# Gate and up products of a gated layer as seven half-size products for eight, in a two-block transformer kernel

## What is computed

```python
def swiglu_ffn(h, w1, w3, w2):
    return (jax.nn.silu(h @ w1) * (h @ w3)) @ w2

    # D_MODEL = 1024, SEQ = 512, D_FF_2 = 2816, two layers
    h = h + swiglu_ffn(rmsnorm(h, norm_ffn_g[layer]), ffn_w1[layer], ffn_w3[layer], ffn_w2[layer])
```

## Time and profile before

| | |
|---|---|
| median of 3 runs | 1737.45 us (1736.9 to 1738.46) |
| span of the profiled execution | 1736.2 us |
| PE busy | 1723.5 us, 99% of the span |
| DVE busy | 817.1 us, 47% |
| ACT busy | 688.5 us, 40% |
| POOL busy | 740.6 us, 43% |
| first gated layer, its stretch on the chain | 359.04 us |
| second gated layer, the same | 342.74 us |

### The profile page before, as it was taken

The page is one execution under the profiler, slowest core; times in us unless marked ns, Lnnn a source line. Parts: engine busy times, 40 slices in busy tenths (PEclk is TensorE's granted clock), DMA queues, the critical chain, the costliest instruction groups (busy, mean ns, idle before and its releaser), DMA issues.

```text
span 1736.2 us, 23746 instructions
## 1 busy us (share of the span) xinstructions
PE 1723.5 (99%) x8050; PEld 1418.5 (82%) x8050; DVE 817.1 (47%) x1457; ACT 688.5 (40%) x1041; POOL 740.6 (43%) x329
## 2 busy tenths in 40 slices
PE   9999999999999999999999999999999999999998
PEld 7877778888888788888888888888888888888887
DVE  5655565333333678532332335566665523323425
ACT  5566553222222434632322224565655432322324
POOL 3232325444446297444354353442424353443441
PEclk9999999999999999999999999999999999999999
DMA  7442223322222133233233233231212332332231
GB/s 199 113 102 79 73 65 117 98 97 97 97 97 97 61 116 107 84 101 97 85 109 97 85 109 97 74 97 48 87 58 74 97 110 85 98 107 85 97 96 49
DMA packets 153686, 162.25 MB, mean 93 GB/s; under 512 B 10628, under 2 KB 114680, under 8 KB 153632
## 3 DMA queue, kind: packets, MB, share of 16 engines
q1 hardware_dynamic: 149167, 158.66, 29.7%
q10 hardware_dynamic: 4464, 2.89, 0.5%
HBM read 157.84 MB, written 3.67 MB: 93 GB/s over the span
## 4 chain that ended last, share of the span: by engine, by line
PE 95%; DVE 2%; ACT 1%; issue 0%; DMA 0%; SPq 0%; DVEq 0%; ACTq 0%
PE ps L1295 83%; PE ps L1316 2%; PE ps L1751 1%; PE ps L1643 1%; PE ps L1324 1%; PE ps L1514 1%; PE ps L1533 1%; DVE ps L2279 1%; PE ps L1426 0%; PE ps L1420 0%; PE ps L1784 0%; PE ps L1497 0%; PE ps L1430 0%; PE ps L1742 0%; PE ps L1498 0%
## 5 line engine op out<-in xcount | busy, mean ns | idle before, releaser
L640 POOL TENSOR_TENSOR wlo<-raw,whi 128x1024 fp32r<-128x1024 f32 x228 | 550.2, 2425 | 765.9 <-ACT whi L730 750.9
L1295 PE MATMUL ps<-h_hi,wlo 128*128 128x512 f32 x1376 | 546.1, 397 | 0.8 <-DVE gv L2045 0.3
L1295 PE MATMUL ps<-h_hi,whi 128*128 128x512 f32 x1376 | 536.6, 390 | 0.0
L1295 PE MATMUL ps<-h_lo,whi 128*128 128x512 f32 x1376 | 536.2, 390 | 0.0
L730 ACT ACTIVATE whi<-raw 128x1024 fp32r<-128x1024 f32 x282 | 292.7, 1055 | 503.7 <-PE ps L1295 495.1
L1295 PE MATMUL ps<-m_hi,wlo 128*128 128x512 f32 x800 | 314.5, 393 | 0.0
L1295 PE MATMUL ps<-m_hi,whi 128*128 128x512 f32 x800 | 311.5, 389 | 0.0
L1295 PE MATMUL ps<-m_lo,whi 128*128 128x512 f32 x800 | 311.4, 389 | 0.0
L1295 PEld LDWEIGHTS ps<-h_hi,whi 128*128 128x128 f32 x1376 | 258.3, 188 | 55.1
L1295 PEld LDWEIGHTS ps<-h_hi,wlo 128*128 128x128 f32 x1376 | 258.5, 188 | 54.2 <-issue 1.6
L1295 PEld LDWEIGHTS ps<-h_lo,whi 128*128 128x128 f32 x1376 | 258.6, 188 | 51.1 <-issue 0.5
(11 more groups left out here) (311 smaller groups left out, 1621.1 us busy)
## 6 DMA issues: line engine op xcount, KB each, us to landing
raw<-in_ffn_w SPq DMA_DIRECT2D x264, 256.0 KB, 2.8
raw<-in_w_ff SPq DMA_DIRECT2D x128, 256.0 KB, 2.8
raw<-in_hg_w_in SPq DMA_DIRECT2D x64, 256.0 KB, 3.1
raw<-in_w_in SPq DMA_DIRECT2D x40, 256.0 KB, 5.2
raw<-in_cp_w_in SPq DMA_DIRECT2D x24, 256.0 KB, 2.9
raw<-in_w_out SPq DMA_DIRECT2D x16, 256.0 KB, 2.9
raw<-in_cp_w_out SPq DMA_DIRECT2D x16, 256.0 KB, 2.9
raw<-in_hg_w_out SPq DMA_DIRECT2D x16, 256.0 KB, 2.9
```

The source lines that it names most:

```text
L640: pool.tensor_tensor(wlo[:, u % RING, :, :], raw[:, u % RING, :, :], whi[:, u % RING, :, :].bitcast(F32), ALU.subtract).then_inc(unit_lo, 1)
L1295: mm = pe.matmul(ps[:, b, :], wt[:, s, a, m * P:(m + 1) * P], xt[:, kts[a], :], start=starts and a == 0 and i == 0, stop=last)
```

## The change

The first two groups stay as they were. From the third on, gate and up of each group are a block each (18 blocks per layer). A block multiplies a 1024 x 256 weight matrix with 1024 x 512 tokens. Both are cut in half both ways, and with Strassen's algorithm (Winograd's form) seven half-size products give what eight gave. Each product has a contraction of 4 tiles, 128 features and 256 tokens: 12 matmuls of 128 x 256, 84 for a block where 48 of 128 x 512 stood.

- Tokens: normalised once, ahead of the first drain (`normed_tokens`), and three or four differences and sums of halves made, split into `t_hi`, `t_lo` and into parts of `m_hi`, `m_lo`, `h_hi`, `h_lo` (the old contents are done with by then).
- Weights: DVE makes four sums for each block (`weight_sum`) and now the seven low parts (`low`, 128 x 512 each). ACT makes the seven high parts. POOL makes only the low parts of the down weights (`down_low`). High and low parts stand in 12 slots of 128 x 512.
- Sums of the products: banks 0 to 3 take one product each in turn; ACT copies the first (`y1`), DVE adds the others from PSUM into `u2`, `u3`, `u4`, `gate` and `ghid` in pieces of 128 x 256. The fifth product is accumulated in PSUM onto the first.
- Down: two groups' down products are summed in PSUM (`down_pair`), so that `xT` is added to once for two groups; the group left over goes alone at the end.
- The norm's matmuls move ahead, to the middle of the second unit of the first group, and ACT's work for the norm ahead of its unit copies.

```diff
+FORMS = 7
+TAGS = ("y1", "u2", "u3", "p5", "c11", "c12", "c21")
+SUM_OF = {1: 2, 2: 3, 3: 1, 5: 4}
+HALF = SEQ // 2
+SLOTS = 12
+BLOCKS = 2 * (GLU_GROUPS - 2)
+PAIRS_IN_LOOP = 3
+LATER_UNITS = 8 + 2 * BLOCKS + 4 * (PAIRS_IN_LOOP + 1)
+N_LOOP, N_TURN = 2 * FORMS + 1, 4 * FORMS + 8
...
+def block_banks(j):
+    at = [(b - j) % 4 for b in (0, 1, 2, 3, 0, 1, 2)]
+    return [((tag, j), b) for tag, b in zip(TAGS, at)]
...
+                def down_low(n0, d0, i=None):
+                    for d in range(8):
+                        n = n0 + d
+                        s = form_slot(layer, n)
+                        u = first + (10 if n0 < N_LOOP else 22) + d // 2
+                        pool.wait_ge(form_hi, at(i, N_TURN, SLOTS_USED * layer + n + 1))
+                        pool.tensor_tensor(lo_slot(s), raw[:, u % RING, d % 2, :], hi_slot(s).bitcast(F32), ALU.subtract)\
+                            .then_inc(down_lo, 1)
...
+                def slot_free(n, i):
+                    if n < 4:
+                        act.wait_ge(tokens_lo, FORMS * layer + 4)
+                    elif n < SLOTS:
+                        act.wait_ge(unit_begun, first + 6 + (n - 4) // 2)
+                    else:
+                        act.wait_ge(form_used, at(i, N_TURN, (SLOTS_USED - 1) * layer + n - SLOTS + 1))
...
@@ -1682,25 +2052,78 @@
...
+                def products(j, slots_before, i=None):
+                    for f in range(FORMS):
+                        s = form_slot(layer, block_slot(j) + f)
+                        b = part_bank(layer, j, TAGS[f])
+                        x_hi, x_lo = rounded_tokens(f)
+                        pe.wait_ge(form_lo, at(i, 4 * FORMS, FORMS * (BLOCKS * layer + j) + f + 1))
+                        if j == 0:
+                            pe.wait_ge(tokens_lo, FORMS * layer + f + 1)
+                        pe.wait_ge(drained[b], part_nth(layer, j, i, TAGS[f]) - 1)
+                        for k in range(4):
+                            for p, (wt, xt) in enumerate(((lo_slot(s), x_hi), (hi_slot(s), x_lo), (hi_slot(s), x_hi))):
+                                begins, ends = k == 0 and p == 0, k == 3 and p == 2
+                                mm = pe.matmul(ps[:, b, 0:HALF], wt[:, k * P:(k + 1) * P], xt[:, k, :],
+                                               start=begins and TAGS[f] != "c11",
+                                               stop=ends, skip_group_check=TAGS[f] == "c11")
+                                if begins and f == 0 and j == 0:
+                                    mm.then_inc(unit_begun, 1)
+                                elif begins:
+                                    mm.then_inc(form_used, 1 if f else slots_before)
+                                if ends:
+                                    mm.then_inc(filled[b], 1)
...
+                group(first, 0, stage, up_tags, 0, 0, (0, 2, 1, 3), 0, n, None, lambda: norm_sum(5 + 2 * layer), 1)
+                group(first, 4, stage, up_tags, 0, 0, (0, 2, 1, 3), 1)
+                products(0, 0)
+                down_pair(FORMS, 0, 0, lambda kt: pe.wait_ge(ghid_lo, 4 * layer + kt + 1))
+                with pe.Fori(0, PAIRS_IN_LOOP) as i:
+                    products(1, 2, i)
+                    for j in range(2, 5):
+                        products(j, 1, i)
+                    down_pair(N_LOOP + 4 * FORMS, 8, i + 1, parts_made(0, i), i)
+                products(TAIL, 2)
+                for j in range(TAIL + 1, TAIL + 5):
...
@@ -2344,44 +2767,274 @@
...
+                def normed_tokens():
+                    for k in range(KT):
+                        dve.scalar_tensor_tensor(out=n1[:, k, :] if k < 4 else ps[:, k, :], in0=xT[:, k, :],
+                                                 scalar=col("norm_ffn_g_2", KT * layer + k), in1=rs[:, :],
+                                                 op0=ALU.mult, op1=ALU.mult).then_inc(tokens_made, 1)
+                    token_step(t3[:, :, :], n2[:, :, HALF:], n1[:, :, HALF:], ALU.subtract, 8)
+                    token_step(t2[:, :, :], t3[:, :, :], n1[:, :, 0:HALF], ALU.add, 9)
+                    token_step(n1[:, :, HALF:], n1[:, :, HALF:], n1[:, :, 0:HALF], ALU.subtract, 10)
+                def last_token_sum():
...
+                def weight_sum(j, k, i=None):
+                    a11, a21, a12, a22 = raw_parts(layer, j)
+                    s1, s2, s3, s4 = (in_tiles(wsums[:, n, :]) for n in range(4))
+                    out, in0, in1, op = {1: (s1, a21, a22, ALU.add), 2: (s2, s1, a11, ALU.subtract),
+                                         3: (s3, a11, a21, ALU.subtract), 4: (s4, a12, s2, ALU.subtract)}[k]
...
+                def low(j, f, i=None):
+                    n = block_slot(j) + f
+                    s = form_slot(layer, n)
+                    dve.wait_ge(form_hi, at(i, N_TURN, SLOTS_USED * layer + n + 1))
+                    if f in SUM_OF:
+                        dve.wait_ge(sums_ready, at(i, 16, 4 * (BLOCKS * layer + j) + SUM_OF[f]))
+                    dve.tensor_tensor(in_tiles(lo_slot(s)), form_source(layer, j, f), in_tiles(hi_slot(s)).bitcast(F32),
+                                      ALU.subtract).then_inc(form_lo, 1)
...
+                def add_p5(j, i=None):
+                    filled_part(j, "p5", i)
...
+                        dve.wait_ge(part_silu, at(i, 4, 2 * group_of(j)))
+                    dve.tensor_tensor(kept[:, 1, HALF:], part(layer, j, "p5"), u3[:, :], ALU.add)
+                    dve.tensor_tensor(u4[:, :], part(layer, j, "p5"), u2[:, :], ALU.add)\
+                        .then_inc(drained[part_bank(layer, j, "p5")], 1)
...
+                def during_gate(x, y, up_before, i=None):
+                    add_c21(up_before, i)
+                    weight_sum(y, 1, i)
+                    weight_sum(y, 2, i)
+                    gated_tile(up_before, i)
+                    low(y, 0, i)
+                    weight_sum(y, 3, i)
+                    hidden_low(up_before, 0, i)
+                    low(y, 1, i)
+                    add_u2(x, i)
+                    hidden_low(up_before, 1, i)
+                    low(y, 2, i)
+                    weight_sum(y, 4, i)
+                    add_u3(x, i)
+                    low(y, 3, i)
+                    add_p5(x, i)
+                    low(y, 4, i)
+                    low(y, 5, i)
+                    low(y, 6, i)
+                    add_c12(x, i)
...
+                def during_down(turn, y, gate_before, i=None):
+                    add_c21(gate_before, i)
+                    weight_sum(y, 1, i)
+                    weight_sum(y, 2, i)
+                    low(y, 0, i)
+                    weight_sum(y, 3, i)
+                    low(y, 1, i)
+                    low(y, 2, i)
+                    weight_sum(y, 4, i)
+                    low(y, 3, i)
+                    low(y, 4, i)
+                    low(y, 5, i)
+                    for k in range(4):
+                        down_tile(turn, k)
+                    low(y, 6, i)
+                    for k in range(4, KT):
+                        down_tile(turn, k)
...
+                dve.wait_ge(rs_ready, 6 + 2 * layer)
+                normed_tokens()
+                up_drain(0)
+                last_token_sum()
+                up_hidden(0)
+                up_lo(0)
+                for f in range(4):
+                    token_lo(f)
+                weight_sum(0, 1)
+                weight_sum(0, 2)
+                low(0, 0)
+                weight_sum(0, 3)
```

602 lines of the change are left out of this document (513 added, 89 removed).

## The result

The changed kernel takes 1725.68 us in the median (1724.18 to 1726.16), the kernel before 1737.5 (1736.9 to 1738.46) on the same chip: a ratio of 0.993, 95% interval 0.9916 to 0.9944. That is 11.8 us gained where 25 were forecast; the profiled span fell from 1736.2 to 1723.4.

The account below looks back on a forecast made before the run. PE's dense matmuls were taken as the bound; 44.9 us gained less 2 x (2 + 3 + 5) = 20 lost left 24.9, so 1736.2 - 24.9 + 1.25 = 1712.5 us, range 1690 to 1732.

Parts of the forecast that it names:

- The matmul, 114.7 ns: Half-size products: 114.7 ns per 256-column matmul, between bounds 111.7 and 120.0; 36 blocks gain 44.9 us.
- rival (a): Half-size products: matmul overhead is fixed, 120.0 ns each; gain 28.8 us, 7 lost per layer, 1722.6 us; chance 0.17.
- DVE in the dense blocks, 2 us a layer: Dense blocks: DVE needs 9.9 us against PE's 9.63, so PE loses 2 us per layer (0 to 6).
- the light fourth block: Block before a down pair: only 9 DVE operations, so DVE's lag from the dense blocks is taken away there.
- Rival (c): Dense blocks: DVE bounds each at 11.2 us, its operations taking their full 0.69 and 0.41 us; 1748 us; chance 0.10.
- POOL beside DVE at the down pair, 3 us a layer: Down pairs: DVE takes turns with POOL's low parts; 0.8 us lost at each of four, 3 per layer (0 to 7).
- The layer's start, 5 us a layer: Layer heads: token work beside POOL's three low parts delays the first drain; 5 us lost per layer (0 to 9).
- (b): Whole kernel: stalls of only 1 or 2 us per layer, matmuls of 111.7 to 114.7 ns; 1691 to 1696 us; chance 0.14.
- (d): Layer starts and down pairs at their upper bounds, 9 and 7 us per layer; 1728.5 us; chance 0.12.
- (e): Half-size products: the weight load shows in each matmul, a block costs 16 us or more; 1917 us and up; chance 0.02.
- What would show it: Signs: matmul starts 115, 120 or 190 ns apart, PE's named waits, DVE operations over 1.2 us beside POOL's.

Follow-up runs that it names:

- e3: Changed kernel with half-size products cut to 244 of 256 columns in the first gated layer, 192 in the second, computation partly left out: 1710.82 us.
- e4: Changed kernel plus useless 128x512 DVE operations, two (second layer: four) in each of four blocks a turn: the 62.1 us turn grew by 3.5 and 9.2 us.
- e6: Changed kernel with the second gated layer's norm sum 12 matmuls later: 1726.31 us, ratio 0.9937 to the kernel before the change.

## Why the prediction was wrong, point by point

- **The matmul, 114.7 ns: the step that failed.** It measured 120.0, the upper of its two bounds and rival (a). The gain before losses is 28.8 us, not 44.9: 16.1 us too much, more than the whole error of 13.2. The prediction had seen both readings of 226.67 ns and chose between them by the float32 stream of L1635, whose fixed part is 3 ns. That row speaks of another kind of matmul. The nearer row was the fp32r one itself, 13.3 ns over its columns, and the only open question whether these go with the columns. The other row taken as a bound gives 111.7 ns, and 111.6 was measured, but for narrower matmuls.
- **DVE in the dense blocks, 2 us a layer: measured 0.** The forecast set DVE's 9.9 us against 9.63. Against 10.08 they fit, as the text of (a) says. With blocks of 9.52 (e3) a debt appeared where the prediction had it, at the down pair and in the tail, but the text let the light fourth block take the lag away. DVE did catch up there; the lag had by then gone on through ACT and POOL into the transfer, a path that the text did not have. The distance of 0.60 us held, as two operations with waits of their own in a dense block show, in answer to the earlier trace rows:

```profile
818.09 0.68 DVE L2904 TENSOR_TENSOR m_lo<-ghid,m_hi 128x512 fp32r<-128x512 f32 x1
818.69 0.68 DVE L2837 TENSOR_TENSOR wlo<-wsums,whi 128x512 fp32r<-128x512 f32 x1
```

  Rival (c) is out, but e4 shows how near it stood.
- **POOL beside DVE at the down pair, 3 us a layer: measured 0** by the first down pairs of the loop (21.79 us each); in e3 0.7 to 1.2 for each of three, by the transfer's route. The text had half of POOL's eight low parts, 5.2 us, beside the down pair. In the turn of the loop they are

```profile
898.14 7.20 POOL L908 TENSOR_TENSOR wlo<-raw,whi 128x512 fp32r<-128x512 f32 x5 [51.13 <-ACT whi L1386]
905.30 3.81 POOL L908 TENSOR_TENSOR wlo_more<-raw,whi_more 128x512 fp32r<-128x512 f32 x3
```

  and the down pair begins at 906.91: 2.2 us of their 11.0 fall into it, the rest into the light block, which has the room.
- **The layer's start, 5 us a layer: 7.7 and 8.6.** The case with POOL's three parts came out within 1 us in the first layer: three operations of POOL taking turns with the tiles, a drain over at 747.6 (748.5 in the text), PE waiting 4.7 us (4.9). What was missing: the half clock behind that wait, 3.0 us, and in the second layer the norm. The text took the parts of its sum as ready half-way through the second unit, which was read from the first layer; in the second PE waited for them. By e6 that wait is not a loss of its own: the head's time is set by `rs` and DVE's work behind it.
- **The sum.** 28.8 less 16.3 is 12.5 us gained; the span shows 12.8, the medians 11.8. Of the forecast's losses of 20 us half (loop and down pairs) did not come, and the heads took 6.3 more than their 10.
- **The rivals.** (a) gave 1722.6 by the right cause, 3 us low because it took 14 us of losses where the heads took 16.3 and the span shows 16.0. (b), (c), (d) and (e) did not happen; (d) had the heads nearly right (9) and the down pairs wrong.
- **What would show it** named the right signs: the distance of starts, and DVE operations over 1.2 us beside one of POOL in the first 30 us of a layer. It didn't name the clock.

## What to carry to other kernels

When a change cuts an instruction in half, half its price is a question, not a fact: 13.3 ns beside the columns are 6% of a 512-column matmul and 11% of a 256-column one, and Strassen's seven for eight (12.5% fewer products) left 7.4% here; cutting the products of 256 columns in two again gained nothing. Where the one kind of row that is at hand can't split fixed from variable, make the forecast for both and let the chances, not a neighbouring kind of instruction, decide. Work that a helper engine does beside a busy DVE is not free: at a tight place it can be cheaper to let DVE do it itself than to have POOL next to it, and moving the order about only moves the wait.
